# Building the slot-to-token table of a routed expert layer: 32 one-hot products in place of 32 scattered writes

## The reference, cut to what matters

```python
counts = jnp.bincount(flat_e, length=N_EXPERTS)
start = jnp.cumsum(counts) - counts
padded = ((counts + MOE_BLOCK - 1) // MOE_BLOCK) * MOE_BLOCK
pend = jnp.cumsum(padded)
pstart = pend - padded
dest = pstart[se] + (jnp.arange(n_assign) - start[se])
rows = jnp.zeros((n_rows, h.shape[1]), h.dtype).at[dest].set(h[stok])
block_e = jnp.minimum(jnp.searchsorted(pend, jnp.arange(n_blocks) * MOE_BLOCK, side='right'), N_EXPERTS - 1)
```

## Time and profile before

| | |
|---|---|
| median of 3 runs | 2628.35 us |
| lowest and highest run | 2627.71 and 2632.11 us |
| profiled execution, from first to last instruction | 2631.2 us (no time of its own beside this span is given) |
| TensorE busy (matmul) | 2182.8 us, 83% |
| VectorE busy | 1414.4 us, 54% |
| ScalarE busy | 1110.2 us, 42% |
| GpSimd busy | 310.3 us, 12% |
| mean granted TensorE clock | 0.924 of full |

### The profile page before, as it was taken

One profiled execution on the slowest core, in us unless ns is written; L12 is line 12 of the kernel. 1 busy time (PEld: TensorE's weight loads), 2 busy tenths in 40 slices (PEclk: granted clock), 3 DMA queues, 4 the chain that ended last, 5 costly groups with the idle time before them and its releaser, 6 DMA issues. The chain is left out here.

```text
span 2631.2 us, 29505 instructions
## 1 busy us (share of the span) xinstructions
PE 2182.8 (83%) x9771; PEld 1642.8 (62%) x9772; DVE 1414.4 (54%) x2372; ACT 1110.2 (42%) x1586; POOL 310.3 (12%) x380
## 2 busy tenths in 40 slices
PE   4999999868969687785999219999999999999950
PEld 4764444357447676675888107777777777777740
DVE  4832581044358567584444527466647847354548
ACT  6101111013227566574222017566648847454432
POOL 0002331025020110000000220000000000000022
PEclk9999999979869899898999559999999999999985
DMA  7023433173651431502443057477668967445649
GB/s 220 34 78 136 168 136 116 51 263 128 260 142 46 100 71 43 112 1 71 140 140 125 17 208 296 197 273 311 250 244 308 368 248 300 186 187 203 252 169 377
DMA packets 129203, 458.84 MB, mean 174 GB/s; under 512 B 26192, under 2 KB 42720, under 8 KB 114784
## 3 DMA queue, kind: packets, MB, share of 16 engines
q1 hardware_dynamic: 98512, 345.28, 37.6%
q0 software_dynamic: 19952, 69.51, 7.1%
q10 hardware_dynamic: 10656, 43.00, 4.0%
HBM read 342.09 MB, written 115.65 MB: 174 GB/s over the span
## 5 line engine op out<-in xcount | busy, mean ns | idle before, releaser
L1532 DVE TENSOR_TENSOR w_gate_lo<-w_gate_raw,w_gate_hi 128x2048 fp32r<-128x2048 f32 x64 | 146.3, 2287 | 180.0 <-ACT w_gate_hi L1487 180.0
L895 DVE CUSTOM_DVE_ANT_0 scores<-c_bank,alibi 128x512 f32<-128x512 f32 (+3 forms) x320 | 175.4, 607 | 109.1 <-PE c_bank L993 108.9
L488 PE MATMUL a_bank<-w_in_chunk,hT 128*128 128x512 f32 x512 | 222.1, 596 | 0.7 <-ACT hT L266 0.7
L488 PE MATMUL a_bank<-hT,w_in_chunk 128*128 128x512 f32 x512 | 220.6, 593 | 0.0
L300 ACT ACTIVATE proj_out<-a_bank 128x512 f32<-128x512 f32 x64 | 38.2, 597 | 398.1 <-PE a_bank L488 387.8
L488 PEld LDWEIGHTS a_bank<-w_in_chunk,hT 128*128 128x128 f32 x512 | 128.8, 252 | 92.6 <-issue 62.8
L1007 PE MATMUL c_bank<-v_head,map_T 128*128 128x128 f32 x1088 | 152.0, 288 | 41.6 <-ACT map_T L951 41.6
L1575 PE MATMUL m_bank<-w_gate_hi,rows_T_hi 128*128 128x512 f32 x392 | 155.0, 395 | 24.1 <-DVE rows_T_lo L1536 24.1
L1613 PE MATMUL m_bank<-w_down_hi,hidden_T_hi 128*128 128x512 f32 x392 | 161.2, 411 | 16.5 <-ACT hidden_T_hi L1509 16.5
L488 PEld LDWEIGHTS a_bank<-hT,w_in_chunk 128*128 128x128 f32 x512 | 97.1, 190 | 120.8 <-issue 120.7
L1007 PEld LDWEIGHTS c_bank<-v_head,map_T 128*128 128x128 f32 x1088 | 135.9, 198 | 57.2 <-ACT map_T L951 57.2
(11 more groups left out here) (370 smaller groups left out, 4429.1 us busy)
## 6 DMA issues: line engine op xcount, KB each, us to landing
w_gate_raw<-in_w_gate_dram SPq DMA_DIRECT2D x32, 2048.0 KB
w_up_raw<-in_w_up_dram SPq DMA_DIRECT2D x32, 2048.0 KB
w_down_raw<-in_w_down_dram SPq DMA_DIRECT2D x32, 2048.0 KB
rows_d<-rows_out ACTq DMA_DIRECT2D x50, 512.0 KB, 10.5
rows_d<-zero_rows POOLq DMA_DIRECT2D x34, 512.0 KB
x_tile<-in_x_dram SPq DMA_DIRECT2D x16, 512.0 KB
w_in_chunk<-in_w_in_dram POOLq DMA_DIRECT2D x4, 2048.0 KB, 19.1
qT_d<-xn_tile SPq DMA_DIRECT2D x32, 256.0 KB
```

What stands on the lines that cost most here:

```text
L488: last = pe.matmul(bank[4 + n % PB][:], lhsT, rhs, start=kt == 0, stop=kt == KT - 1)
L895: dve.tensor_tensor_reduce(S[:, s, m, c * BANK:c * BANK + w], bank[n % 4][:, 0:w], bias[:, h % 2, x0:x0 + w], 1.0, -BIG, ALU.add, ALU.max, ...
L1532: dve.tensor_tensor(wlo[w][:, s], raw[w][:, s], whi[w][:, s], ALU.subtract).then_inc(lo_done[w], 1)
```

## The change: one-hot products, and block tables by partition

The slot of a token is split into its row in the block (`dest` and 127) and its block (`dest` shifted right by 7). For each of the 32 columns of `dest` VectorE writes a one-hot row of 128 columns (`slot_row_onehot`) and one of 64 columns in which the one is replaced by the token's number (`slot_block_token`). TensorE multiplies the two, with the tokens as the contracted dimension, and sums all 32 products in one bank of PSUM: that is the table, rows on partitions and blocks along the columns. Empty slots come out as zero, as before. The zero fill, the scattered writes, the read-back, the cast and the turn leave, with the DRAM tensor.

The block tables are made with the block number on the partitions: partition b compares all 32 experts with b (`below`), one reduction gives two numbers for each partition (`block_facts`), and two small products turn them onto partition 0 in PSUM. The last steps then run on partition 0 alone. They stand behind the one-hots in VectorE's order.

```diff
-        tok = sb("token_id", [P, NT], I32)
-        zero = sb("zero_ids", [NBLK, P], I32)
+        tok_i, tok = sb("token_id_i", [P, NT], I32), sb("token_id", [P, NT])
+        place_i = sb("slot_place_i", [P, 2, 2, NT], I32)
+        place = sb("slot_place", [P, 2, 2, NT])
+        at_row = sb("slot_row_onehot", [P, 2, NT, P], F32R)
+        at_block = sb("slot_block_token", [P, 2, NT, NBLK], F32R)
+        per_row = sb("block_facts", [P, 2])
...
             def _(pool):
-                pool.memset(zero[:], 0).then_inc(c_step, 1)
+                pool.tensor_copy(tok[:], tok_i[:]).then_inc(c_ready, 1)
...
-                pool.wait_ge(zero_st, 16)
-                pool.wait_ge(dest_ready, 2)
-                for k in range(2):
-                    for i in range(NT):
-                        pool.indirect_dma_start(d["slot_token"], bass.IndirectOffsetOnAxis(ap=dest[:, k, i:i + 1], axis=0),
-                                                tok[:, i:i + 1], None).then_inc(scattered, 16)
-                pool.wait_ge(scattered, 16 * 2 * NT)
-
-            @block.sync
-            def _(sp):
-                sp.wait_ge(c_step, 3)
-                sp.dma_start(d["slot_token"].rearrange("(b p) o -> b (p o)", p=P), zero[:]).then_inc(zero_st, 16)
-                sp.wait_ge(scattered, 16 * 2 * NT)
-                sp.dma_start(idi[:], d["slot_token"].rearrange("(b p) o -> b (p o)", p=P)).then_inc(ids_in, 16)
...
-                pe.wait_ge(ids_f, 1)
-                pe.transpose(bank[2][:, 0:NBLK], idf[:], ident[0:NBLK, 0:NBLK]).then_inc(ids_T, 1)
+                pe.wait_ge(facts_ready, 1)
+                for f in range(2):
+                    last = pe.matmul(bank[3][0:1, f * P:(f + 1) * P], per_row[:, f:f + 1], ident[:], start=True, stop=True)
+                last.then_inc(facts_psum, 1)
+
+                for k in range(2):
+                    for i in range(NT):
+                        pe.wait_ge(slots_ready, 2 * (k * NT + i + 1))
+                        last = pe.matmul(bank[2][:, 0:NBLK], at_row[:, k, i], at_block[:, k, i],
+                                         start=k == 0 and i == 0, stop=k == 1 and i == NT - 1)
+                last.then_inc(ids_psum, 1)
...
+                step(dve.tensor_scalar(filled[:], nblk[:], 0.0, None, ALU.is_gt))
+                step(dve.tensor_tensor_scan(order[:], ones[:, 0:NE], filled[:], 0.0, ALU.mult, ALU.add))
+
+                step(dve.tensor_scalar(below[:, 0], pend[:], tok[:, 0:1], None, ALU.is_le))
+                step(dve.tensor_tensor(below[:, 0], below[:, 0], filled[:], ALU.mult))
+                step(dve.tensor_scalar(below[:, 1], order[:], tok[:, 0:1], None, ALU.is_le))
+                dve.tensor_reduce(per_row[:], below[:], AX.X, ALU.add).then_inc(facts_ready, 1)
+
                 for k in range(2):
                     step(dve.tensor_tensor(M[:], Ak[k], rank[:], ALU.mult))
                     step(dve.tensor_reduce(df[:], M[:], AX.X, ALU.add))
-                    dve.tensor_copy(dest[:, k], df[:, :, 0]).then_inc(dest_ready, 1)
-                    dve.wait_ge(dest_ready, k + 1)
...
-                step(dve.tensor_tensor(big[:], over(pend, NBLK), upto(NBLK), ALU.is_le))
-                step(dve.tensor_tensor(big[:], big[:], over(filled, NBLK), ALU.mult))
-                step(dve.tensor_reduce(bf[:, 0:NBLK], big[:], AX.X, ALU.add))
...
-                step(dve.tensor_tensor(big[:, 0:NE], over(order, NE), upto(NE), ALU.is_le))
-                step(dve.tensor_reduce(bf[:, META_ID:META_ID + NE], big[:, 0:NE], AX.X, ALU.add))
-                step(dve.tensor_copy(meta[:], bf[:]))
-
-                dve.wait_ge(ids_in, 16)
-                dve.tensor_copy(idf[:], idi[:]).then_inc(ids_f, 1)
-                dve.wait_ge(ids_T, 1)
+                    step(dve.tensor_copy(dest[:, k], df[:, :, 0]))
+                    step(dve.tensor_scalar(place_i[:, k, 0], dest[:, k], P - 1, None, ALU.bitwise_and))
+                    step(dve.tensor_scalar(place_i[:, k, 1], dest[:, k], 7, None, ALU.logical_shift_right))
+                    step(dve.tensor_copy(place[:, k], place_i[:, k]))
+                    for i in range(NT):
+                        dve.tensor_scalar(at_row[:, k, i], count[:], place[:, k, 0, i:i + 1], None, ALU.is_equal).then_inc(slots_ready, 1)
+                        dve.tensor_scalar(at_block[:, k, i], count[:, 0:NBLK], place[:, k, 1, i:i + 1], tok[:, i:i + 1],
+                                          ALU.is_equal, ALU.mult).then_inc(slots_ready, 1)
+
+                dve.wait_ge(facts_psum, 1)
+                step(dve.tensor_copy(bf[0:1, META_BLOCKS:META_BLOCKS + 1], pend[0:1, NE - 1:NE]))
+                step(dve.tensor_copy(bf[0:1, META_EXPERTS:META], order[0:1, NE - 1:NE]))
+                step(dve.tensor_scalar(df[0:1, 0], order[0:1, NE - 1:NE], -1.0, None, ALU.add))
+                step(dve.tensor_scalar(bf[0:1, 0:NBLK], bank[3][0:1, 0:NBLK], df[0:1, 0, 0:1], None, ALU.min))
+                step(dve.tensor_copy(bf[0:1, META_ID:META_ID + NE], bank[3][0:1, P:P + NE]))
+                step(dve.tensor_copy(meta[0:1], bf[0:1]))
+
+                dve.wait_ge(ids_psum, 1)
                 step(dve.tensor_copy(ids[:, 0:NBLK], bank[2][:, 0:NBLK]))
```

More of the change, by code:

```diff
@@ L1243, in route @@
         sem = ctx.enter_context(phase_semaphores(nc))
-        bank = [ctx.enter_context(nc.psum_tensor(f"r_bank{i}", [P, BANK], F32)) for i in range(3)]
+        bank = [ctx.enter_context(nc.psum_tensor(f"r_bank{i}", [P, BANK], F32)) for i in range(4)]
         count_i, count = sb("count_i", [P, P], I32), sb("count", [P, P])
@@ L1257, in route @@
         base = sb("rank_base", [P, NT + 1, NE])
-        big = sb("compare", [P, NBLK, NE])
+        big = sb("compare", [P, NE, NT])
+        below = sb("below", [P, 2, NE])
         nblk, pend, sbase, rank = sb("n_blocks", [P, NE]), sb("block_end", [P, NE]), sb("slot_base", [P, NE]), sb("rank", [P, NT, NE])
@@ L1261, in route @@
         filled, order = sb("filled", [P, NE]), sb("filled_order", [P, NE])
-        idf = sb("ids_f", [NBLK, P])
-        idi = sb("ids_i", [NBLK, P], I32)
         c_step, c_ready, r_step, exp_in, exp_done, any_ready, pref_done = (
             sem(n) for n in ("c_step", "c_ready", "r_step", "exp_in", "exp_done", "any_ready", "pref_done"))
-        zero_st, dest_ready, scattered, ids_in, ids_f, ids_T = (
-            sem(n) for n in ("zero_stored", "dest_ready", "scattered", "ids_loaded", "ids_f_ready", "ids_T"))
+        slots_ready, ids_psum, facts_ready, facts_psum = (
+            sem(n) for n in ("slots_ready", "ids_psum", "facts_ready", "facts_psum"))
         with nc.Block() as block:
@@ L1307, in _ @@
             def _(pe):
-                pe.wait_ge(c_ready, 2)
+                pe.wait_ge(c_ready, 3)
                 pe.wait_ge(any_ready, 1)
@@ L1320, in _ @@
                 wide = lambda t, n: t.to_broadcast([P, NT, n])
-                dve.wait_ge(c_ready, 2)
+                dve.wait_ge(c_ready, 3)
                 def first_max(val, n, mxt, idx, out, tmp):
@@ L1380, in _ @@
                     step(dve.tensor_reduce(df[:], M[:], AX.X, ALU.add))
-                    dve.tensor_copy(dest[:, k], df[:, :, 0]).then_inc(dest_ready, 1)
-                    dve.wait_ge(dest_ready, k + 1)
-                over = lambda t, n: t[:].rearrange("p (o e) -> p o e", o=1).to_broadcast([P, n, NE])
-                upto = lambda n: count[:, 0:n].rearrange("p (b o) -> p b o", o=1).to_broadcast([P, n, NE])
-                step(dve.tensor_scalar(filled[:], nblk[:], 0.0, None, ALU.is_gt))
@@ L1387, in _ @@
-                step(dve.tensor_tensor_scan(order[:], ones[:, 0:NE], filled[:], 0.0, ALU.mult, ALU.add))
-                step(dve.tensor_tensor(big[:], over(pend, NBLK), upto(NBLK), ALU.is_le))
-                step(dve.tensor_tensor(big[:], big[:], over(filled, NBLK), ALU.mult))
-                step(dve.tensor_reduce(bf[:, 0:NBLK], big[:], AX.X, ALU.add))
-                step(dve.tensor_copy(bf[:, META_BLOCKS:META_BLOCKS + 1], pend[:, NE - 1:NE]))
-                step(dve.tensor_copy(bf[:, META_EXPERTS:META], order[:, NE - 1:NE]))
@@ L1394, in _ @@
-                step(dve.tensor_scalar(df[:, 0], order[:, NE - 1:NE], -1.0, None, ALU.add))
-                step(dve.tensor_scalar(bf[:, 0:NBLK], bf[:, 0:NBLK], df[:, 0, 0:1], None, ALU.min))
-                step(dve.tensor_tensor(big[:, 0:NE], over(order, NE), upto(NE), ALU.is_le))
-                step(dve.tensor_reduce(bf[:, META_ID:META_ID + NE], big[:, 0:NE], AX.X, ALU.add))
-                step(dve.tensor_copy(meta[:], bf[:]))
-                dve.wait_ge(ids_in, 16)
-                dve.tensor_copy(idf[:], idi[:]).then_inc(ids_f, 1)
@@ L1705, in hybrid_layer @@
         "cos": dram("cos_d", [NB, P, GB, NCH]), "sin": dram("sin_d", [NB, P, GB, NCH]),
-        "slot_token": dram("slot_token_d", [NBLK * P, 1], I32), "rows": dram("rows_d", [NBLK + 2, P, D]),
+        "rows": dram("rows_d", [NBLK + 2, P, D]),
```

11 lines of the change are left out of this document (5 added, 6 removed).

## The result

| | before | changed |
|---|---|---|
| median of four runs each, us | 2630.23 (2627.71 to 2633.72) | 2600.45 (2598.93 to 2605.58) |
| ratio, 95% interval | | 0.9885 (0.9871 to 0.9899) |
| span of the profiled execution, us | 2631.2 | 2597.2, at a time of 2598.93 |
| `rank` to `slot_ids`, us | 52.74 | 21.37 |

The changed kernel is faster by 30.2 us by that ratio (26.6 to 33.9, times 2630.23); 2595.4 with a range of 2590.5 to 2601 was forecast. The last row of the table is my yardstick for everything that follows. It is the time from the start of the last addition into `rank`, up to which both programs do the same work, to the start of the cast that writes `slot_ids`; call it the stretch. In the kernel before, it goes from 1486.47 to 1539.21.

The account below looks back on a forecast made before the run. GpSimd's chain of 32 scattered writes was taken to bound stage `route`: 48.7 us leave, 1.4 + 4.5 + 11.7 + 1.4 = 19.0 us are added, `slot_ids` 33.0 earlier. Taken from the median: 2595.4 us, range 2590.5 to 2601.

Parts of the forecast that it names:

- 1. block facts: Block-table steps on VectorE ahead of the slots (`filled`, scan, comparisons, product, reduction): 1.4 us added.
- 2. slots, twice: Product, reduction, cast, mask, shift and cast back on VectorE, 2.25 us for each half: 4.5 us added.
- 5. six steps: Last VectorE steps on partition 0 before `slot_ids`, including the last one-hot's own end: 1.4 us added.
- item 3: The 64 one-hots on VectorE, 0.367 us a pair with the second scalar at no charge: 11.7 us for 32 pairs.
- rival B: Dear one-hot pairs on VectorE, one column a cycle or the second scalar paid: 16.5 us, 2600.2 us in all; chance 0.10.
- Rival A: Cheap one-hot pairs on VectorE, scalar fetched under the forerunner: 8 us, 2591.7 us in all; chance 0.13.
- Rival C: VectorE one-hots held as beside a working GpSimd, 0.48 us each: 19.0 us more, 2614.4 us in all; chance 0.02.
- Rival D: VectorE one-hots held by GpSimd through the shared memory way, 1.70 us each: slower than before, 2694 us; chance 0.01.
- Rival E: Gain given back because the experts' first products wait for something tied to absolute time; within 0.2% of 2628; chance 0.02.
- Item 4: TensorE's 32 products follow a pair behind the one-hots, starting every 0.22 to 0.39 us; lag at the end under 1 us.
- The gather's worry: First gather of `experts` may take 2.94 us instead of 1.01 after a long pause; costed at nothing, some 19 us cover.
- The comparisons ... were hidden: VectorE's old block-table comparisons of 2048 and 1024 columns lay under GpSimd's writes and cost nothing before the change.

Follow-up runs that it names:

- half_writes: Kernel before the change with 16 of its 32 scattered writes left out; 2614.71 us, stretch 33.01 us.
- one_scalar: Changed kernel with the token's number left out of the 64-column one-hots, so one per-partition scalar instead of two; 2595.18 us, stretch 19.44 us.
- batched: Changed kernel with both halves' slots made at once, one-hots by wide instructions and the token number multiplied in by ScalarE; 2590.41 us, ratio 0.9863, stretch 15.73 us.
- onehots_old_tables: Changed kernel with block tables made by the old long comparisons, placed behind the one-hots; 2609.18 us, ratio 0.9907, stretch 29.77 us.
- writes_beside: Changed kernel with 16 unused scattered writes by GpSimd added beside the one-hots; 2598.2 us, stretch 25.58 us.
- writes_new_tables: Changed kernel with the slot table made by the 32 scattered writes and read-back again, block tables still by partition; 2629.03 us, ratio 0.9999, stretch 50.86 us.
- changed_again: The changed kernel itself run once more, six runs; 2599.16 us, ratio 0.9876, stretch 21.37 us.
- products_late: Changed kernel with TensorE's 32 products all waiting for the last one-hot, so they run back to back; 2605.93 us, stretch 27.39 us.

## Why the prediction was right, and where it was off

The mechanism was the one forecast, and the size nearly so. The writes' chain bounded the stage (`half_writes`, 1.23 us each), VectorE's chain took its place, no other engine joined in, and the stages behind moved along.

Step by step, the sum's numbers against the differences of starts in the trace:

| term | forecast | measured |
|---|---|---|
| 1. block facts | 1.4 | 1.39 |
| 2. slots, twice | 4.5 | 4.58 |
| 3. 32 pairs | 11.7 | 13.41 |
| 5. six steps | 1.4 | 1.27 |
| sum | 19.0 | 20.65 |

- **The mis-sized term is item 3**, in its words "the second scalar at no charge". The step from the 128-column one-hot to the next was 0.20 as forecast; that from the 64-column one was 0.22 where 0.167 was forecast. 32 times 0.053 is 1.7, the whole gap. `one_scalar` shows it directly: without the second scalar the one-hot takes 0.251, with it 0.305. My reading of rows 7 gave the first scalar 0.05; no row had a second, and taking it at nothing was a choice that no row backed.
- **Half of rival B** is what came. It named two things, one column a cycle or a paid second scalar, and priced them together. In `one_scalar` 128 columns take 0.282 and 64 take 0.251, 0.5 ns a column as rows 6 and 7 gave, so the first half is refuted and the second true. **Rival A** falls: no scalar is fetched for free.
- The estimate by the table of the Trainium skill ("VectorE: DVE Perf Modes", the section on the TRN2 errata) was 0.22 us a pair; the runs show 0.42, and with one scalar fewer 0.36. The measurement decides. The same section of the Trainium skill says below its table that this row comes out too low for a single instruction and that the measured fixed part is about 150 cycles, not 58. By that, as an estimate at half a cycle a column, 32 columns with an immediate take 0.173 and 2048 take 1.223, where rows 6 and 7 have 0.18 and 1.227; the prediction used the lower figure. The advice of the Trainium skill there against many small instructions still points the right way: `batched` replaces 64 of them on VectorE by 10 wide ones (and 32 on ScalarE), and its stretch is 5.6 us shorter, 4.5 of it without the slots.
- **Rival C** rested on a row of 0.448 taken beside the writes. `onehots_old_tables` has the same instruction at 0.25 with GpSimd silent. But `writes_beside` shows that not even running writes would have held most one-hots at that length (the median stayed 0.304), so the price in rival C, 0.48 for each of the 64, was an exaggeration as well.
- **Rival D** didn't come, yet its mechanism is real: beside busy GpSimd instructions one-hots of 5.5 us are measured. What kept it away is only that GpSimd has nothing to do there, as the argument said.
- **Rival E** didn't come: the first expert product starts 31.3 us earlier and takes 0.76 as against 0.77, and the same rise of the clock follows. In the first 10 us from that product the granted clock is 0.74 (before 0.78), in the next 10 it is 1.00 in both.
- Item 4 held: the products ended at 1507.10 and 0.22 was their pace. The gather's worry (2.94 like the first write) was groundless: it took 1.08. `writes_new_tables` shows why the 2.94 was no price of a first write: without VectorE's comparisons beside it that write takes 1.13. I had read contention as a cold start.
- **"The comparisons ... were hidden"** was not quite so. They held GpSimd's writes by 3.5 us. It changed nothing in my sum, since I took the writes' measured span, but it would have misled anyone who priced 32 writes by the median row (32 x 1.26 = 40.3; the span of starts and the last one were 43.8).
- **The base.** Of the traces' difference of 34.0 us in span, 31.4 lie in the stretch. The other 2.6 arise between the first expert product and the last copy of that stage, which is 2.6 us shorter in the changed kernel's trace (967.5 and 964.8 from the second split of rows to `last_copy`); the same span is 960.9 to 971.4 us in the nine other traces, whose experts' code is the same, and 968.7 in `changed_again`, the very same program. That is a scatter between executions, so I don't credit it to the change. With 31.4 as the effect and the median of 2630.23 the time would be 2598.8; the measured 2600.45 lies 1.6 beside it, within the spread of the runs.
- **How near it was.** The forecast of 2595.4 is 5.1 us below the measured time, and the upper end of the range only 0.5 above it. Of the 5.1, item 3 is 1.6; 1.9 is the base, whose median was 2628.35 when I wrote and 2630.23 in the result; 1.6 is spread. The upper end came from rival B, half of which is refuted, so that the time lies inside the range is in part luck. The stretch, which neither base nor spread touches, was forecast 33.0 shorter and is 31.4 shorter.

Open is what delays the waits in `writes_beside`. So is whether `batched` beats the changed kernel in time as it does in the trace.

## What to carry to other kernels

Price an added train of small instructions by the step from one start to the next, from rows of the same form, and charge each per-partition operand for itself; here only a form with one operand was in the trace, and the second cost about what the first did (0.054 and 0.05 us). Before calling work hidden, look whether the instructions that hide it are longer where the two overlap: the first, odd rows of a series (2.94, 1.86, 1.78 among 0.96) are the sign. And when a cover is taken away, remake what lay under it in the same edit: the long tables cost 3.5 us under the writes and 11.1 without them, 8.4 more than the tables by partition.

## What the runs showed of the hardware

- A `tensor_scalar` in f32 with 64 columns takes 0.251 us with one per-partition scalar and 0.305 with two; with 128 columns and one, 0.277 to 0.282. Followed by one that doesn't wait, each gives way 0.08 us before its end.
- A GpSimd `tensor_scalar` of 128x2048 takes 5.4 us while VectorE runs such instructions, and holds one of them for its whole length (5.5 us). Scattered writes of GpSimd hold them to 0.55 at most, and the held one ends with the write.
- The holding goes both ways: an indirect write that takes 0.96 took up to 2.94 beside VectorE's two-input instructions of 2.29 us, and 1.78 beside one of 1.22. Beside a reduction of 2.29 us, which has one input, it took 0.96.
- Beside a series of scattered writes, TensorE's waits for VectorE in the first half of the one-hots were released in the rhythm of the writes, 1.30 us, and six short steps of VectorE that wait for one another took 5.08 us instead of 1.27. An earlier row of such steps beside the same writes was not delayed. The cause is open.
- Products of 128x128 by 128x64 with their weight loads follow each other in 0.22 us at a granted clock of 0.50, the lower of the two levels (1.2 GHz; `products_late`, 1504 to 1511 us).
